# An mLSTM decoder layer: the output projection's second half of columns one chunk later, and operand transposes between halves of the first gate products

## Chip, cores and metric

One core of one Trainium2 chip. The metric is the device time in microseconds from the start to the end of one execution. The kernel before was run three times: median 2276.28 us.

## What is computed

One decoder layer (DEPTH = 1, so the mixer is the mLSTM), in float32, 2048 tokens of width 1024, then a SwiGLU feed-forward of width 2816:

```python
h = x
u = rmsnorm(h, mix_norm_g)
q, k, v, o_pre, if_pre = split(u @ w_in)                 # 8 heads, q and k of 64, v of 128
C, n, m = scan over chunks of the sequence               # matrix memory, stabilised by a running maximum
y = (merge_heads(_rms(num / max(|den|, exp(-m)))) * norm_g * sigmoid(o_pre)) @ w_out
h = h + y
u = rmsnorm(h, ffn_norm_g)
h = h + (silu(u @ w_gate) * (u @ w_up)) @ w_down
```

## The kernel before

Every engine's program is written out by hand, in order, with counting semaphores; no scheduler moves anything. The 2048 tokens are done as two halves of 1024 (`h` = 0, 1), and each half in stages:

- input projections (`project`, L1778), the products of normed rows with `w_in`, stored to HBM;
- the **chunk stage**, a loop over `TILES` = 8 chunks of 128 tokens (L1961 on TensorE, L1510 on VectorE, L990 on ScalarE, L712 on GpSimd);
- the **gate phase**, 11 groups of 14 products `feed(n, q, b)` (L1991), weights against the normed rows of the residual stream;
- the **down phase**, 77 products `drain(e)`.

Float32 precision comes from pairs of numbers: each operand is kept as a high part (a cast on ScalarE) and a low part (a subtraction on VectorE), and each product is three matmuls (low moving, high moving, low weights). The feed-forward products use a seven-product scheme over 2x2 blocks (`P1` to `P7`), so that besides the rows themselves some sums of rows are wanted as operands.

**A chunk on TensorE** (L1962 to L1977): `spread` (mask and decay arguments), `scores`, `weights` (its last four matmuls are transposes of k), then the first half of `out_tile(c - 2, 1)`, `turn_heads(c - 1)` (eight transposes of the normed heads), the second half of `out_tile(c - 2, 1)`, `state_sums`, `outputs`, `turn_v(c + 1)`, and `out_tile(c - 1, 0)`. `out_tile(c, jj, k0, k1)` is the output projection of chunk `c` for columns `512 * jj` on, 24 matmuls for all eight `k`, into bank `jj`.

**The heads of a chunk on the other engines.** After `outputs`, VectorE runs `head_scale_a`/`head_scale_b` (a chain of small operations that ends with `hrow`, L1489), TensorE turns `hrow`, VectorE multiplies with the gate (`gate_heads`, `og`, L1438), ScalarE casts that to `hg_hi` (L978), VectorE subtracts to `hg_lo` (L1443). `hg_hi` and `hg_lo` have two buffers. `add_out(c, jj)` (L1498) adds a finished `out_tile` to the residual rows `res`; when both column halves of a chunk are in, ScalarE sums squares (`norm2_sum`), GpSimd stores the rows to HBM (`store_h`, L710), and VectorE norms them (`norm2_rows`, L1150; for rows 0 to 5 it waits for that store).

**From the chunk stage to the gate phase** (L1979 to L1989, then inside `feed_group`, L2018, for the first group). The gate phase wants 16 operand units, `turn_unit(st + 1, n)`: units 0 to 3 are chunks 0 to 3 of the rows, units 4 to 15 are four triples made of row sums, parts A (4 + 4 transposes), B (4 + 4) and C (4). VectorE's `sum_early` (L1167, L1169) and GpSimd's `sum_late` (L632, L636) make the sums. A unit is transposed by TensorE (L1723), cast by ScalarE (`op_hi`, L781) and subtracted by VectorE (`op_lo`, L1174). Two PSUM places alternate, so from unit 4 on a transpose waits for an `op_lo` two units back:

```python
                if n >= 6 or (stage == 0 and n >= 2):
                    pe.wait_ge(op_lo_done, at + n - 1)
                elif n >= 4:
                    pe.wait_ge(op_lo_done, at + n - 2)
                elif stage % 2 and n == 3:
                    pe.wait_ge(op_lo_done, at + 1)
```

The first group's products 0 to 3 need units 0 to 3 only (`op_lo_done` 4); product 4 needs all parts B. The orders of VectorE and ScalarE in this stretch are L1568 to L1596 and L1021 to L1047. `feed_hi`/`feed_low` prepare a product's weights in `ring`, `feed_sums` their sums.

Of the kernel before, what the change touches and what calls it, by code (L numbers as in the profile page):

```python
# [5 lines left out]
F32 = mybir.dt.float32  # L6
# [79 lines left out]

def made_of(i, part=0):

    return i if i < 4 else 4 + 3 * (i - 4) + part


def mlstm_layer(nc, x, mix_norm_g, ffn_norm_g, w_gate, w_up, w_down, w_in, b_if, norm_g, w_out, out):
# [8 lines left out]
    with ExitStack() as ctx:  # L101
# [23 lines left out]
        r_q = region(32 * KB)  # L125
# [41 lines left out]
        hg_hi = [place(f"hg_hi{s}", r_q + 8 * KB * s, [P, KD, P], F32R) for s in range(2)]  # L167
        hg_lo = [place(f"hg_lo{s}", r_q + 8 * KB * s + 4 * KB, [P, KD, P], F32R) for s in range(2)]
# [205 lines left out]
        def part_of(stage, n):  # L374
            return ("BCA", "ABC")[stage % 2][(n - 4) % 3]

        def unit_for(stage, i, part):
            return made_of(i, ("BCA", "ABC")[stage % 2].index(part))
# [62 lines left out]
        def _(sp):  # L441
# [25 lines left out]
            for h in range(HALVES):  # L467
# [73 lines left out]
                sp.wait_ge(n_done, h * 8 + 8)  # L541
# [60 lines left out]
        def _(pool):  # L602
# [35 lines left out]
            for h in range(HALVES):  # L638
# [68 lines left out]
                def store_h(i):  # L707
                    pool.wait_ge(res_added, h * 16 + 2 * i + 2)
# [3 lines left out]
                for c in range(TILES):  # L712
                    if c >= 2:
                        store_h(c - 2)
                    squares(c)
                store_h(6)
                sum_late(st + 1, 0)
                sum_late(st + 1, 1)
                store_h(7)
                sum_late(st + 1, 2)  # L720
# [38 lines left out]
        def _(act):  # L759
# [42 lines left out]
            for h in range(HALVES):  # L802
# [171 lines left out]
                def hg_high(c):  # L974
                    act.wait_ge(hg_done, h * 8 + c + 1)
                    if c >= 2:
                        act.wait_ge(outp_done, h * 16 + 2 * (c - 2) + 2)
                    nc.scalar.copy(hg_hi[c % 2][:, :, :], og[c % 2][:, :, :]).then_inc(hghi_done, 1)  # L978

                def norm2_sum(i):  # L980
                    n = (st + 1) * TILES + i
                    act.wait_ge(res_added, h * 16 + 2 * i + 2)
# [7 lines left out]
                for c in range(TILES):  # L990
# [9 lines left out]
                    if c >= 2:  # L1000
                        norm2_sum(c - 2)
# [21 lines left out]
                feed_hi(0, 2)  # L1023
                norm2_sum(6)
                hg_high(7)
                act.wait_ge(outp_done, h * 16 + 15)
# [4 lines left out]
                act.wait_ge(hglo_done, h * 8 + 8)  # L1031
                norm2_sum(7)
                act.wait_ge(outp_done, h * 16 + 16)
                feed_hi(0, 3)
                for n in range(4, OP_UNITS):
                    op_hi(st + 1, n)
# [94 lines left out]
        def _(dve):  # L1131
# [102 lines left out]
            for h in range(HALVES):  # L1234
# [206 lines left out]
                def hg_low(c):  # L1441
                    dve.wait_ge(hghi_done, h * 8 + c + 1)
                    nc.vector.tensor_tensor(hg_lo[c % 2][:, :, :], og[c % 2][:, :, :],  # L1443
                                            hg_hi[c % 2][:, :, :].bitcast(F32), ALU.subtract).then_inc(hglo_done, 1)
# [659 lines left out]
```

## Time and profile before

| | |
|---|---|
| median of 3 runs | 2276.28 us (2270.1 to 2278.3) |
| the profiled execution, its own time | 2272.74 us |
| span of its instructions | 2271.1 us |
| TensorE matmuls busy | 2160.6 us (95%) |
| VectorE busy | 1459.3 us (64%) |
| ScalarE busy | 922.6 us (41%) |
| GpSimd busy | 280.4 us (12%) |
| mean granted TensorE clock | 0.980 |

The span runs from the first to the last instruction; the execution's own time is 1.64 us more. A matmul's end is modelled: a row of 0.39 us is followed by the next 0.23 us after its start when nothing is in the way, so "busy" is not the rate. Idle time stands in brackets behind a row, with what ended it. A granted clock of 1.0 is 2.4 GHz and 0.5 is 1.2 GHz.

### The profile page before, as it was taken

The page shows a single profiled execution, that of the slowest core. Times are in us where ns is not written, and L with a number is a line of the kernel's source. Part 1 is how long each engine was busy: PE and PEld are TensorE (multiplying, and loading weights), DVE is VectorE, ACT ScalarE, POOL GpSimd, SP SyncE. Part 2 cuts the span into 40 slices and gives each one's busy share as a digit, 9 for nine tenths or more (in the row PEclk, how much of TensorE's full clock was granted, in tenths as well). Part 3 has the DMA queues.
Part 4 walks back from the last instruction along what each step waited for, and adds up shares of the span by engine and source line. Part 5 has one row for each costly group of instructions (what it writes and reads, how often), then busy time and mean ns, then how long its engine had stood idle before and what let it go on. Part 6 is the DMA issues. An engine that isn't in the chain of part 4 may idle for free.

```text
span 2271.1 us, 29460 instructions
## 1 busy us (share of the span) xinstructions
PE 2160.6 (95%) x10440; PEld 1791.1 (79%) x10440; DVE 1459.3 (64%) x2274; ACT 922.6 (41%) x1670; POOL 280.4 (12%) x373
## 2 busy tenths in 40 slices
PE   5999989989999999999989999899799999999999
PEld 4778868867888888888867888688588888887887
DVE  7755456777565656579667553677766565656764
ACT  5433653334333333445434346533343333333443
POOL 3111110120010101100021111111201010101000
PEclk8999989999999999999999999899899999999999
DMA  4323372212323233864413334623032323257443
GB/s 140 96 90 112 102 263 95 97 47 74 113 93 115 92 115 127 298 228 114 149 63 107 107 104 138 218 102 103 19 112 98 111 97 111 97 179 247 148 120 117
DMA packets 200288, 281.56 MB, mean 124 GB/s; under 512 B 12912, under 2 KB 131696, under 8 KB 200176
## 3 DMA queue, kind: packets, MB, share of 16 engines
q1 hardware_dynamic: 171696, 183.07, 25.7%
q0 software_dynamic: 28480, 97.02, 12.1%
q8 instruction: 68, 1.11, 0.2%
q14 instruction: 44, 0.36, 0.0%
HBM read 197.73 MB, written 82.31 MB: 123 GB/s over the span
## 4 chain that ended last, share of the span: by engine, by line
PE 87%; DVE 7%; ACT 2%; issue 2%; DMA 1%; SPq 0%; POOL 0%; DVEq 0%; ACTq 0%; POOLq 0%
PE ps L2011 12%; PE ps L2013 12%; PE ps L2014 12%; PE ps L1802 6%; PE ps L1806 6%; PE ps L1804 6%; PE ps L2058 6%; PE ps L2062 6%; PE ps L2060 6%; PE ps L1716 2%; PE ps L1718 2%; PE ps L1717 2%; PE ps L1723 1%; PE ps L1924 1%; DVE u_lo L1174 1%
## 5 line engine op out<-in xcount | busy, mean ns | idle before, releaser
L1561 DVE TENSOR_TENSOR ring<-raw_f,ring 128x512 fp32r<-128x512 f32 x308 | 213.4, 694 | 190.0 <-ACT ring L1019 188.8
L2011 PE MATMUL ps<-u_lo,ring 128*128 128x512 f32 x704 | 275.1, 391 | 4.3 <-DVE u_lo L1174 4.3
L1019 ACT CAST ring<-raw_f 128x512 fp32r<-128x512 f32 x308 | 190.6, 622 | 212.0 <-PE ps L2014 196.8
L2013 PE MATMUL ps<-u_hi,ring 128*128 128x512 f32 x704 | 274.2, 389 | 0.0
L2014 PE MATMUL ps<-u_hi,ring 128*128 128x512 f32 x704 | 274.0, 389 | 0.0
L2058 PE MATMUL ps<-ring,ring 128*128 128x512 f32 x616 | 241.2, 392 | 3.3 <-DVE ring L1635 3.2
L2060 PE MATMUL ps<-ring,ring 128*128 128x512 f32 x616 | 240.4, 390 | 0.0
L2062 PE MATMUL ps<-ring,ring 128*128 128x512 f32 x616 | 240.2, 390 | 0.0
L2011 PE MATMUL ps<-t_op,ring 128*128 128x512 f32 x528 | 207.3, 393 | 5.9 <-DVE ring L1561 5.9
L2013 PE MATMUL ps<-t_op,ring 128*128 128x512 f32 x528 | 207.0, 392 | 0.0
L2014 PE MATMUL ps<-t_op,ring 128*128 128x512 f32 x528 | 206.9, 392 | 0.0
L1057 ACT CAST ring<-g_in 128x512 fp32r<-128x512 f32 x154 | 95.6, 621 | 222.3 <-PE ps L2062 210.3
L729 POOL DMA_DIRECT2D ops_hbm<-kept x154 | 83.3, 541 | 784.5 <-DVE kept L1654 584.9
L1629 DVE TENSOR_TENSOR ring<-g_in,ring 128x512 fp32r<-128x512 f32 x154 | 106.1, 689 | 112.7 <-ACT ring L1057 112.7
L1186 DVE TENSOR_TENSOR pring<-raw,pring 128x512 fp32r<-128x512 f32 x132 | 90.9, 691 | 128.1 <-ACT pring L798 127.3
L1802 PE MATMUL ps<-u_lo,pring 128*128 128x512 f32 x384 | 152.8, 398 | 9.0 <-ACT pkept L888 4.5
L1649 DVE TENSOR_TENSOR kept<-ps,kept 128x512 f32<-128x512 f32 x132 | 90.9, 688 | 109.3 <-PE ps L2014 109.3
L2011 PEld LDWEIGHTS ps<-u_lo,ring 128*128 128x128 f32 x704 | 132.5, 188 | 32.5 <-DVE u_lo L1174 5.1
L2014 PEld LDWEIGHTS ps<-u_hi,ring 128*128 128x128 f32 x704 | 132.3, 188 | 27.5
L2013 PEld LDWEIGHTS ps<-u_hi,ring 128*128 128x128 f32 x704 | 132.4, 188 | 27.1
L1804 PE MATMUL ps<-u_hi,pring 128*128 128x512 f32 x384 | 151.5, 395 | 0.0
L1806 PE MATMUL ps<-u_hi,pring 128*128 128x512 f32 x384 | 151.4, 394 | 0.0
(218 smaller groups left out, 4276.6 us busy)
## 6 DMA issues: line engine op xcount, KB each, us to landing
ops_hbm<-kept POOLq DMA_DIRECT2D x154, 256.0 KB, 2.4
g_in<-ops_hbm SPq DMA_DIRECT2D x154, 256.0 KB, 2.7
raw<-in_ml_w_in_dram SPq DMA_DIRECT2D x24, 1024.0 KB, 5.3
proj_hbm<-pkept POOLq DMA_DIRECT2D x96, 256.0 KB, 2.7
raw_f<-in_ffn_w_gate_dram SPq DMA_DIRECT2D x44, 512.0 KB, 4.7
raw_f<-in_ffn_w_up_dram SPq DMA_DIRECT2D x44, 512.0 KB, 4.7
b<-in_ffn_w_down_dram SPq DMA_DIRECT2D x88, 256.0 KB, 4.9
x_in<-in_x_dram SPq DMA_DIRECT2D x16, 512.0 KB, 5.9
```

The lines of the kernel that those rows point to most:

```text
L1019: nc.scalar.copy(four(ring[slot][:, 0, :]), feed_source(q, s)).then_inc(w_hi_done, 1)
L1561: nc.vector.tensor_tensor(four(ring[slot][:, 1, :]), feed_source(q, s), four(ring[slot][:, 0, :].bitcast(F32)), ALU.subtract).then_inc(w_l ...
L1629: nc.vector.tensor_tensor(ring[e % 3][:, 1, :], g_in[e % 4][:, :], ring[e % 3][:, 0, :].bitcast(F32), ALU.subtract).then_inc(ea_lo_done, 1)
L1802: pe.matmul(banks(bank), w[:, 0, now], moved(kind, 1, k), start=(fresh and k == 0), stop=False, skip_group_check=True)
L1804: pe.matmul(banks(bank), w[:, 0, now], moved(kind, 0, k), start=False, stop=False, skip_group_check=True)
L1806: last = pe.matmul(banks(bank), w[:, 1, now], moved(kind, 0, k), start=False, stop=(k == 3), skip_group_check=True)
L2011: pe.matmul(banks(bank), wh, moved(kind, 1, k), start=(fresh and k == 0), stop=False, skip_group_check=True)
L2013: pe.matmul(banks(bank), wh, moved(kind, 0, k), start=False, stop=False, skip_group_check=True)
L2014: last = pe.matmul(banks(bank), wl, moved(kind, 0, k), start=False, stop=(k == 3), skip_group_check=True)
L2058: pe.matmul(banks(bank + j), a[:, 0, now], w[:, 1, :], start=(fresh and n == 0), stop=False, skip_group_check=True)
L2060: pe.matmul(banks(bank + j), a[:, 0, now], w[:, 0, :], start=False, stop=False, skip_group_check=True)
L2062: last = pe.matmul(banks(bank + j), a[:, 1, now], w[:, 0, :], start=False, stop=(n == GROUPS - 1), skip_group_check=True)
```

## The change

The second half of columns of the output projection, `out_tile(c, 1)`, runs three chunks behind instead of two; for this the gated heads get a third pair of buffers (`hg_hi`, `hg_lo`, 8 KB per partition, behind `v1`), and every wait that counted `outp_done` or `res_added` goes by the new order, written as a table:

```diff
+OUT_ORDER = ([(0, 0), (1, 0)] + [pair for c in range(3, 8) for pair in ((c - 3, 1), (c - 1, 0))]
+             + [(5, 1), (6, 1), (7, 0), (7, 1)])
+def out_at(h, c, jj):
+    return h * 16 + OUT_ORDER.index((c, jj)) + 1
...
-        r_q = region(32 * KB)
+        r_q = region(32 * KB + 64)
...
+        hg_at = [r_q, r_q + 8 * KB, r_q + 24 * KB + 64]
...
-            return ("BCA", "ABC")[stage % 2][(n - 4) % 3]
+            return ("BCA", "BAC")[stage % 2][(n - 4) % 3]
```

TensorE in the chunk loop and after it:

```diff
-                    if c >= 2:
-                        out_tile(c - 2, 1, 0, 4)
+                    if c >= 3:
+                        out_tile(c - 3, 1, 0, 4)
...
-                out_tile(6, 1, 0, KD)
+                out_tile(5, 1, 0, KD)
                 turn_heads(7)
...
                 turn_unit(st + 1, 0)
                 turn_unit(st + 1, 1)
-                out_tile(7, 0, 0, KD)
+                out_tile(6, 1, 0, KD)
                 pe.wait_ge(hg_done, h * 8 + 8)
                 turn_unit(st + 1, 2)
+                out_tile(7, 0, 0, KD)
+                out_tile(7, 1, 0, 4)
                 turn_unit(st + 1, 3)
-                out_tile(7, 1, 0, KD)
+                out_tile(7, 1, 4, KD)
+                turn_unit(st + 1, 4)
```

In the first gate group the remaining units stand between halves of products 0 to 3 (`feed` takes a range of `k`):

```diff
-                        if first and q == 1:
-                            turn_unit(st + 1, 4)
-                            turn_unit(st + 1, 5)
...
+                        if first and q < 4:
+                            feed(n, q, b, 0, 2)
+                            turn_unit(st + 1, 5 + 2 * q)
+                            feed(n, q, b, 2, 4)
+                            turn_unit(st + 1, 6 + 2 * q)
+                            continue
                         if first and q == 4:
-                            for n_ in range(12, OP_UNITS):
-                                turn_unit(st + 1, n_)
+                            turn_unit(st + 1, 13)
+                            turn_unit(st + 1, 14)
+                            turn_unit(st + 1, 15)
```

Before product 4 TensorE now waits for 14 `op_lo`, before product 6 for 15. VectorE after the loop:

```diff
-                add_out(6, 1)
+                add_out(5, 1)
                 gate_heads(7)
                 hg_low(7)
-                norm2_rows(6)
-                op_lo(st + 1, 0)
-                op_lo(st + 1, 1)
+                norm2_rows(5)
+                add_out(6, 1)
                 sum_early(st + 1, 0)
                 sum_early(st + 1, 1)
+                norm2_rows(6)
                 add_out(7, 0)
+                op_lo(st + 1, 0)
+                op_lo(st + 1, 1)
+                sum_early(st + 1, 2)
                 op_lo(st + 1, 2)
                 op_lo(st + 1, 3)
-                sum_early(st + 1, 2)
                 add_out(7, 1)
+                op_lo(st + 1, 4)
                 norm2_rows(7)
+                feed_low(0, 3)
+                op_lo(st + 1, 5)
                 sum_early(st + 1, 3)
-                feed_low(0, 3)
```

ScalarE's order follows (a `norm2_sum(5)` ahead of `hg_high(7)`, `op_hi` of unit 4 ahead of `norm2_sum(7)`); GpSimd stores rows 5, 6 and 7 later; SyncE's load of the third and fourth gate weight blocks waits for `out_tile(5, 1)` instead of the last chunk's `outputs`. The instructions of every kind stay as many as they were; no DMA is added.

**TensorE, chunk 2 of the first half** (`qkc` is q and k, `hrow` the heads of chunk 1, `wo` the output weights). Before:

```order
L1881 MATMUL ps<-qkc_91 128x128 x8
L1891 MATMUL ps<-wint,pick 128x128 x4
L1895 MATMUL ps<-ident,qkc_91 128x128 x4
L1716 MATMUL ps<-wo_1_110,hg_hi_103 128x512
L1717 MATMUL ps<-wo_0_109,hg_hi_103 128x512
L1718 MATMUL ps<-wo_0_109,hg_lo_105 128x512
...
L1931 MATMUL ps<-ident,hrow 128x128 x8
```

and now:

```order
L1897 MATMUL ps<-qkc_91 128x128 x8
L1907 MATMUL ps<-wint,pick 128x128 x4
L1911 MATMUL ps<-ident,qkc_91 128x128 x4
L1947 MATMUL ps<-ident,hrow 128x128 x8
L1922 MATMUL ps<-v_0_96,kw 64x129 x8
L1936 MATMUL ps<-state,qw 128x129 x8
L1940 MATMUL ps<-v_0_96,dmat 128x129 x8
L1956 MATMUL ps<-ident,vtc 128x128 x8
L1732 MATMUL ps<-wo_1_110,hg_hi_104 128x512
L1733 MATMUL ps<-wo_0_109,hg_hi_104 128x512
L1734 MATMUL ps<-wo_0_109,hg_lo_107 128x512
```

Between the transposes of k and those of the heads stood 12 matmuls of `out_tile(0, 1)`, with 12 more behind the heads; now the heads follow directly, and the next `wo` rows are `out_tile(1, 0)`.

**TensorE, the first gate products** (`ring` holds weights, `res`, `t_second` the rows and sums of a unit). Before, behind product 0:

```order
L1723 MATMUL ps<-ident,res 128x128 x8
L1723 MATMUL ps<-ident,t_second_212 128x128 x4
L1723 MATMUL ps<-ident,res 128x128 x4
L2011 MATMUL ps<-u_lo,ring_122 128x512
L2013 MATMUL ps<-u_hi,ring_122 128x512
L2014 MATMUL ps<-u_hi,ring_122 128x512
...
L1723 MATMUL ps<-ident,res 128x128 x12
L1723 MATMUL ps<-ident,t_second_213 128x128 x4
L1723 MATMUL ps<-ident,res 128x128 x4
```

and now, from the middle of product 0 on:

```order
L1739 MATMUL ps<-ident,res 128x128 x8
L2031 MATMUL ps<-u_lo,ring_123 128x512
L2033 MATMUL ps<-u_hi,ring_123 128x512
L2034 MATMUL ps<-u_hi,ring_123 128x512
...
L1739 MATMUL ps<-ident,res 128x128 x4
L2031 MATMUL ps<-u_lo,ring_124 128x512
L2033 MATMUL ps<-u_hi,ring_124 128x512
L2034 MATMUL ps<-u_hi,ring_124 128x512
...
L1739 MATMUL ps<-ident,t_second_215 128x128 x4
L1739 MATMUL ps<-ident,res 128x128 x4
```

Where two or three units stood in a row between whole products of 12 matmuls, one unit now stands behind every six matmuls.

**VectorE, from the last `add_out` of the stage on** (L1174, now L1186, is `op_lo`; L1167 and L1169, now L1179 and L1181, are `sum_early`; L1498, now L1510, is `add_out`; the `nv` rows and the one behind them are the norm of rows 7). Before:

```order
L1498 TENSOR_TENSOR res<-ps,res 128x512
L1136 TENSOR_SCALAR nv<-nv 128x1
L1141 TENSOR_SCALAR nv<-nv 128x1
L1144 SCALAR_TENSOR_TENSOR nv<-nv 128x1
L1150 SCALAR_TENSOR_TENSOR xn_0_115<-res,nv,gain_114 128x1024
L1167 TENSOR_TENSOR res<-xn_0_115,res 128x512
L1169 TENSOR_TENSOR t_second_215<-xn_0_115,res 128x512
L1561 TENSOR_TENSOR ring_124<-raw_f_118,ring_124 128x512
L1174 TENSOR_TENSOR u_lo<-ps,u_hi 128x8x128
L1174 TENSOR_TENSOR t_op<-ps,t_op 128x2x4x128
```

and now, from `op_lo` of units 2 and 3 on:

```order
L1186 TENSOR_TENSOR u_lo<-ps,u_hi 128x8x128 x2
L1510 TENSOR_TENSOR res<-ps,res 128x512
L1186 TENSOR_TENSOR t_op<-ps,t_op 128x2x4x128
L1148 TENSOR_SCALAR nv<-nv 128x1
L1153 TENSOR_SCALAR nv<-nv 128x1
L1156 SCALAR_TENSOR_TENSOR nv<-nv 128x1
L1162 SCALAR_TENSOR_TENSOR xn_0_117<-res,nv,gain_116 128x1024
L1573 TENSOR_TENSOR ring_126<-raw_f_120,ring_126 128x512
L1186 TENSOR_TENSOR u_lo<-ps,u_hi 128x8x128
L1179 TENSOR_TENSOR res<-xn_0_117,res 128x512
L1181 TENSOR_TENSOR t_second_217<-xn_0_117,res 128x512
```

`op_lo` of unit 4 now stands ahead of the norm of rows 7, and that of unit 5 ahead of the last sums.

## Rows read from the trace of the kernel before

**Rows 1.** The page: span, busy time, chain by engine

```profile
span 2271.1 us, 29460 instructions
...
PE 2160.6 (95%) x10440; PEld 1791.1 (79%) x10440; DVE 1459.3 (64%) x2274; ACT 922.6 (41%) x1670; POOL 280.4 (12%) x373
...
PE 87%; DVE 7%; ACT 2%; issue 2%; DMA 1%; SPq 0%; POOL 0%; DVEq 0%; ACTq 0%; POOLq 0%
```

**Rows 2.** Stretches: length, PE, PEld, DVE, ACT, POOL busy (count), clock, DMA share, GB/s

```profile
361.88:382.12 20.24, 20.24 (x148) 17.22 (x147) 14.57 (x28) 7.39 (x18) 2.50 (x2) 1.00 0.30 106
...
462.20:524.00 61.80, 45.98 (x242) 37.94 (x240) 44.66 (x59) 23.21 (x36) 13.54 (x10) 0.94 0.04 17
...
529.70:600.00 70.30, 70.30 (x311) 58.18 (x310) 46.98 (x72) 28.23 (x49) 7.61 (x14) 1.00 0.36 113
1581.50:1643.20 61.70, 45.76 (x242) 37.74 (x240) 44.56 (x58) 23.14 (x36) 13.52 (x10) 0.93 0.04 18
```

**Rows 3.** Timeline of PE behind the loop: start, duration, what, [idle before, releaser]

```profile
473.84 0.61 PE L1716 MATMUL ps<-wo,hg_hi 128*128 128x512 f32 x1 [3.38 <-DVE hg_lo L1443]
474.25 0.63 PE L1717 MATMUL ps<-wo,hg_hi 128*128 128x512 f32 x1
...
477.24 0.51 PE L1718 MATMUL ps<-wo,hg_lo 128*128 128x512 f32 x1
...
483.55 1.09 PE L1723 MATMUL ps<-ident,res 128*128 128x128 f32 x8 [1.49 <-DVE u_lo L1174]
484.40 0.48 PE L1716 MATMUL ps<-wo,hg_hi 128*128 128x512 f32 x1
...
492.26 0.50 PE L2011 MATMUL ps<-u_lo,ring 128*128 128x512 f32 x1 [2.15 <-DVE u_lo L1174]
...
503.53 0.63 PE L1723 MATMUL ps<-ident,res 128*128 128x128 f32 x4 [3.75 <-issue]
504.62 1.83 PE L1723 MATMUL ps<-ident,res 128*128 128x128 f32 x8 [0.46 <-DVE t_op L1174]
506.24 1.06 PE L1723 MATMUL ps<-ident,t_second 128*128 128x128 f32 x4
...
523.94 0.47 PE L2011 MATMUL ps<-t_op,ring 128*128 128x512 f32 x1 [2.94 <-DVE ring L1561]
```

**Rows 4.** Waits of PE, 462 to 530: in total, times, longest

```profile
PE ps L1723 <- DVE u_lo L1174: 2.2, 2, 1.5
...
PE ps L1723 <- DVE t_op L1174: 1.4, 3, 0.5
```

**Rows 5.** Timeline of PE in chunk 2

```profile
344.96 0.48 PE L1716 MATMUL ps<-wo,hg_hi 128*128 128x512 f32 x1
...
356.31 0.47 PE L1716 MATMUL ps<-wo,hg_hi 128*128 128x512 f32 x1
```

**Rows 6.** Timeline of ACT in chunk 2

```profile
343.10 2.17 ACT L955 ACTIVATE dmat<-ps,colt 128x128 f32<-128x128 f32 x8 [1.23 <-PE ps L1869]
350.14 1.05 ACT L978 CAST hg_hi<-og 128x1024 fp32r<-128x1024 f32 x1 [4.87 <-DVE og L1438]
```

**Rows 7.** Timeline of DVE: chunk 2, the end of chunk 7, and behind the loop

```profile
346.05 1.21 DVE L1431 TENSOR_TENSOR dmat<-ps,dmat 128x1024 f32<-128x1024 f32 x1
...
463.73 1.22 DVE L1489 TENSOR_TENSOR hrow<-num,hv 128x1024 f32<-128x1024 f32 x1
...
484.54 0.68 DVE L1167 TENSOR_TENSOR res<-res 128x512 f32<-128x512 f32 x1
...
485.86 1.78 DVE L1167 TENSOR_TENSOR res<-res 128x512 f32<-128x512 f32 x1
...
497.89 1.29 DVE L1150 SCALAR_TENSOR_TENSOR xn<-res,nv,gain 128x1024 f32<-128x1024 f32 x1
...
502.22 1.21 DVE L1174 TENSOR_TENSOR u_lo<-ps,u_hi 128x1024 fp32r<-128x1024 f32 x1
```

**Rows 8.** Landing of the stores of rows to HBM, all 16

```profile
DMA to landing us min/median/max: 2.9/3.9/12.8
```

More of the change, by code:

```diff
@@ L166, in mlstm_layer @@
         num = place("num", r_c + 28 * KB, [P, HEADS, VW], F32)
-        hg_hi = [place(f"hg_hi{s}", r_q + 8 * KB * s, [P, KD, P], F32R) for s in range(2)]
-        hg_lo = [place(f"hg_lo{s}", r_q + 8 * KB * s + 4 * KB, [P, KD, P], F32R) for s in range(2)]
+        hg_at = [r_q, r_q + 8 * KB, r_q + 24 * KB + 64]
+        hg_hi = [place(f"hg_hi{s}", at, [P, KD, P], F32R) for s, at in enumerate(hg_at)]
+        hg_lo = [place(f"hg_lo{s}", at + 4 * KB, [P, KD, P], F32R) for s, at in enumerate(hg_at)]
         wo = [[place(f"wo{jj}_{part}", r_u + 16 * KB * jj + 32 * KB * part, [P, KD, NB], F32R) for part in range(2)]
@@ L1030, in _ @@
                 op_hi(st + 1, 3)
-                act.wait_ge(hglo_done, h * 8 + 8)
+                op_hi(st + 1, 4)
                 norm2_sum(7)
-                act.wait_ge(outp_done, h * 16 + 16)
+                act.wait_ge(outp_done, out_at(h, 7, 1))
                 feed_hi(0, 3)
-                for n in range(4, OP_UNITS):
+                for n in range(5, OP_UNITS):
                     op_hi(st + 1, n)
@@ L1520, in _ @@
                             split_out(1, k)
-                    if c >= 2:
-                        add_out(c - 2, 1)
+                    if c >= 3:
+                        add_out(c - 3, 1)
                     if c:
@@ L1969, in _ @@
                         turn_heads(c - 1)
-                    if c >= 2:
-                        out_tile(c - 2, 1, 4, KD)
+                    if c >= 3:
+                        out_tile(c - 3, 1, 4, KD)
                     state_sums(c)
@@ L2008, in feed @@
                     fresh = kind in ("P1", "P2", "P5")
-                    for k in range(4):
+                    for k in range(k0, k1):
                         wh, wl = ring[slot][:, 0, k * P:k * P + P], ring[slot][:, 1, k * P:k * P + P]
@@ L2015, in feed @@
                                          skip_group_check=True)
-                    last.then_inc(fed, 1)
+                    if k1 == 4:
+                        last.then_inc(fed, 1)
                 def feed_group(n, b, is_second=False):
```

74 lines of the change are left out of this document (35 added, 39 removed).

## The prediction

> **What bounds the kernel now.** I read the page first: TensorE's matmuls are busy for 95% of the span and hold 87% of the chain of work that ended last, VectorE 7% [rows 1]. So time is won only where TensorE stands idle or runs at the lower clock, and VectorE matters where TensorE waits for it. Then the table of stretches [rows 2]: a chunk from the third on takes 20.24 us and TensorE is busy in all of it; the gate phase from 529.70 on too, 311 matmuls in 70.30 us, 0.226 us each. Between them lies the way from chunk stage to gate phase, 462.20 to 524.00, where TensorE is busy for 45.98 of 61.80 us, at a mean clock of 0.94; the second half has the same stretch with 45.76 of 61.70 us. This is the place of the change.
>
> The timeline of that stretch [rows 3] and the waits in it [rows 4] name nine idle times: 3.38 us until the low part of chunk 7's heads is there, 1.49 and 0.74 (together the 2.2 of the waits on `u_lo`), 2.15 ahead of product 0, 3.75 ahead of unit 6, 1.4 in three waits for `t_op`, 2.94 ahead of product 4. Sum 15.8 us. The 3.75 stands as "issue"; by the program unit 6 waits for `op_lo` of unit 4, which is the row that starts at 502.22 and ends at 503.43 [rows 7], just ahead of 503.53. A matmul's row is 0.39 long where the next starts after 0.23, so each idle time costs about 0.16 more than its bracket: nine times, 1.4. There is a lower clock too: after the 3.38 idle eight matmuls stand 0.43 apart instead of 0.23 (0.63 long, 474.25 to 477.24), 1.6 us late; after the 3.75 idle eight transposes take 1.62 us to the next row (504.62 to 506.24), where at 483.55 eight took 0.85, and as many more follow: 1.5 us. That is 2.4 GHz against 1.2 GHz. Together the stretch holds 15.8 + 1.4 + 3.1 = **20.3 us** above its work, per half.
>
> **The change, part by part.**
>
> *Chunk 2 loses its cover.* `out_tile(0, 1)`, 24 matmuls, 5.45 us, leaves chunk 2 and every later one slides by a chunk, so chunks 3 to 7 hold the same work as before and stay at 20.24. In chunk 2 TensorE comes to the heads at 344.96 [rows 5], but the eight exponentials on the decay arguments, whose banks the heads overwrite, end at 343.10 + 2.17 = 345.27 [rows 6]: idle 0.5. The heads themselves are ready. Next check: `out_tile(1, 0)`, at 356.31 before, is reached at about 351.3. It needs the low part of chunk 1's heads: VectorE ends `dmat` at 347.26 [rows 7], gates for 1.2 (348.5), ScalarE casts 1.05 [rows 6] (349.6), VectorE subtracts (350.9). 0.4 us of slack. So 0.5, at least 0.3, and if the chain of heads were 2 us later, 2.5.
>
> *The work behind the loop.* The stretch now starts 5.45 - 0.5 = 5.0 us earlier and holds 5.45 us more. The heads of chunk 7, before ready at 463.73 + 1.22 = 464.95 [rows 7], come 5.0 earlier too, at 460, and TensorE asks for them behind `out_tile(5, 1)` at 462.7. While gate, cast and subtraction run (until about 468.8), TensorE has two units and `out_tile(6, 1)` until 470.7: the **3.38 is gone**, and with it the lower clock behind it.
>
> *Unit 3 and product 0.* Late next is VectorE. After `out_tile(6, 1)` it has an `add_out` (0.68), four sums, the norm of rows 6 (1.29 and its small steps, 2.0), `add_out(7, 0)` and `op_lo` of unit 0 (1.21) before unit 3 may start. The sums take 0.68 each alone and 1.78 where GpSimd works beside them [rows 7], so 2.7 to 4.9 in all. The chain is 7.3 to 9.5 us, from 470.7 to 478.0 to 480.2, with four hand-overs of 0.1 at most 480.6; TensorE is there at 470.7 + 0.85 + 5.45 + 2.72 = 479.8. Idle 0 to 0.8 by this, I take 1.0 since ScalarE's casts of rows sit between. Unit 3 and the last 12 output matmuls then run without a hole, unit 4 too, and `op_lo` of unit 3 is done at about 485.5, when TensorE reaches product 0. **1.49 becomes 1.0, 2.15 becomes 0.**
>
> *Units 5 to 12 between halves of products.* A unit takes 0.85, its cast 1.05, its subtraction 1.21: 3.1, and 3.3 with hand-overs. The unit two behind starts after unit n, six matmuls (1.36), the unit between (0.44 or 0.85), six matmuls: 4.0 or more. So these waits are covered as long as VectorE is free at once. `op_lo` of unit 4 now stands ahead of the norm of rows 7, which takes the **3.75** away with its lower clock; but `op_lo` of unit 5 still stands behind that norm, and unit 7 waits for it: by the same sums VectorE is done at 492.0, TensorE ready at 491.2. Idle 0.9.
>
> *Units 13 to 15 and product 4.* These have no matmuls between them. Unit 13 waits for unit 11: 3.3 against 0.85 + 1.36 + 0.44, idle 0.5. Unit 15 waits for unit 13: 3.3 against 1.7, idle 1.5. Product 4 comes behind the last casts, the first two copies and the weights' low part, and was late by 2.94; now two sums of weights stand ahead of the last two `op_lo`, so I take 3.5.
>
> *Small things.* The first matmul after transposes is 0.48 long instead of 0.39 [rows 3]; four more such changes per half, 0.4. SyncE's load of two weight blocks now waits for the end of `out_tile(5, 1)`, at 462.7, and its blocks are first summed near 498. The store of rows 5 is issued at 464.8 and wanted at 468.8, 4.0 us later; stores land in 3.9 at the median, 12.8 at most [rows 8]. I take 0.3 of wait on VectorE, covered, since the next `add_out` waits until 470.8.
>
> **The sum, per half:** 20.3 taken away; given back 0.5 + 1.0 + 0.9 + 0.5 + 1.5 + 3.5 + 0.4 = 8.3. Gain 12.0, twice 24 us. The profiled execution took 2272.74 us, so 2248.7 against it. The median of the runs is 3.5 us above that execution; halfway between, I predict **2250 us**.
>
> **A rule that speaks against it.** In the trace the eight transposes at 483.55 and the matmuls behind them run at the upper clock, and the two falls came after idle times of more than 3 us [rows 3]. The Trainium skill, "TensorE: Matmul & The Clock Gate", Part 4 (PE-mode transpose), says that transposes do not count as activity for the clock gate the way matmuls do. By that rule groups of six matmuls with transposes between them could run at 1.2 GHz; the time of that is the third rival.
>
> **Rivals.**
>
> 1. *VectorE becomes the bound of the stretch.* It is busy for 44.7 of the 61.8 us, and gets an `add_out` and a norm more: 47.3. My sum squeezes the stretch to 61.7 + 5.0 - 12.0 = 54.7 us, with only 7.4 us of VectorE idle where it had 17. If its chains to ScalarE keep 12.7 us idle, the stretch is 60 and the gain 6.7 per half: **2259**. For it: each `op_lo` waits for a cast. Against: the long idle times of VectorE were caused by ScalarE waiting for whole output tiles, which now come earlier. 20%.
> 2. *The lost cover in chunk 2 and the short slack of the store.* If the heads' chain costs 2.5 in chunk 2 and a store of rows 5 lands after 12.8 us (8.8 late, of which 2 are covered), a half loses up to 8.8: gain 3 per half, **2266**, no change by measure. Against: only one store in 16 was that long. 10%.
> 3. *The lower clock, ending slower.* From unit 3 on, 60 matmuls of output and gate products and 88 transposes are mixed. At 1.2 GHz each of these matmuls costs 0.2 more (12.0 us) and eight transposes 0.77 more (8.5 us): 20 per half, 8 more than the gain, so **2289**. It decides from about 12 us lost per half, that is when more than half of the mixed stretch runs at the lower level. For it: the falls at 474 and 504. Against: both followed idle times of 3.4 and 3.7 us, and none longer than 1.5 is left before unit 15. 4%.
> 4. *All new idle times stay covered*, gain 17 to 20 per half: **2235**. 5%.
>
> **Chances.** My forecast, 2240 to 2259 about 2250, has 61%. A change below 0.5% (11.4 us) can't be told from none in this kernel; from 2276.3 the bounds are 2264.9 and 2287.7. Faster takes the forecast, rival 4, nearly all of rival 1: 83%. Same: rival 2 and the edge of rival 1, 13%. Slower: 4%. The range, 2239 to 2265, leaves out rival 4, rival 3 and most of rival 2.
>
> **What would show it.** Right: the chunk from 341.6 takes about 15.3; no idle time at the first row of `out_tile(7, 0)`; `op_lo` of unit 4 starts about 486.6; product 4 starts about 511 with some 3 us of idle ahead of it; PE's idle time between loop and product 4 is 7 us per half; both halves alike. Wrong: waits of 1 us or more at most of units 5 to 12 (rival 1), matmuls 0.43 apart between 480 and 505 (rival 3), idle ahead of `out_tile(1, 0)` (rival 2).

## The result, and the profile after

| | before | after |
|---|---|---|
| median of the runs | 2273.43 us (2268.7 to 2278.3, 8 runs) | 2282.41 us (2279.26 to 2289.88, 8 runs) |
| the profiled execution | 2272.74 us | 2279.28 us |
| span | 2271.1 us | 2277.5 us |
| mean granted TensorE clock | 0.980 | 0.982 |

The ratio is 1.0039, with a 95% interval of 1.0025 to 1.0054: no faster, 0.4% slower, inside the 0.5% that counts as no change, and above the range of 2239 to 2265. The prediction of 2250 was wrong.

The page of the kernel after: span, busy time, chain by engine.

```profile
span 2277.5 us, 29462 instructions
...
PE 2183.0 (96%) x10440; PEld 1787.0 (78%) x10440; DVE 1458.5 (64%) x2274; ACT 922.8 (41%) x1670; POOL 279.8 (12%) x373
...
PE 87%; DVE 7%; issue 2%; ACT 2%; DMA 2%; SPq 0%; DVEq 0%; ACTq 0%; POOLq 0%
```

Against [rows 1] the same 10440 matmuls are busy for 22.4 us more. Nothing in the change adds a matmul or lengthens one on purpose, and the mean granted clock is no lower (0.982 against 0.980), so the loss is not a wait: each matmul takes longer.

Now the kernel after at the place of the change and behind it. The timeline of PE (TensorE): the first matmul of chunk 2 and of chunk 3, then every idle time above 0.4 us between the loop and product 4, with two of the matmuls behind the first of them.

```profile
344.89 0.39 PE L1882 MATMUL ps<-mask,ident_b 128*128 128x512 bf16 x1
...
359.99 0.39 PE L1882 MATMUL ps<-mask,ident_b 128*128 128x512 bf16 x1
...
486.35 1.09 PE L1739 MATMUL ps<-ident,res 128*128 128x128 f32 x8 [2.81 <-DVE u_lo L1186]
...
487.80 0.63 PE L1734 MATMUL ps<-wo,hg_lo 128*128 128x512 f32 x1
...
490.78 0.54 PE L1732 MATMUL ps<-wo,hg_hi 128*128 128x512 f32 x1
...
499.00 0.66 PE L1739 MATMUL ps<-ident,t_second 128*128 128x128 f32 x4 [0.83 <-DVE u_lo L1186]
...
511.10 0.66 PE L1739 MATMUL ps<-ident,t_second 128*128 128x128 f32 x4 [0.55 <-DVE u_lo L1186]
...
514.56 0.66 PE L1739 MATMUL ps<-ident,res 128*128 128x128 f32 x4 [1.49 <-DVE t_op L1186]
...
518.33 0.69 PE L2031 MATMUL ps<-t_op,ring 128*128 128x512 f32 x1 [3.11 <-DVE ring L1573]
```

The nine idle times of [rows 3], 15.8 us, have become five, 8.8 us. That is the part of the change that the prediction was about, and it came. What came with it stands in the gate and down phases, which the change doesn't touch. First two stretches of 100 us of the kernel before (gate phase, down phase), then the same of the kernel after, and for the change's own place its stretch. The columns are those of [rows 2], and the number in brackets behind the first busy time is that of matmuls started:

```profile
600.00:700.00 100.00, 100.00 (x443) 82.79 (x442) 59.13 (x92) 36.91 (x64) 8.66 (x16) 1.00 0.33 105
940.00:1040.00 100.00, 100.00 (x443) 82.79 (x442) 75.47 (x119) 44.65 (x81) 2.84 (x4) 1.00 0.68 235
```

```profile
600.00:700.00 100.00, 100.00 (x437) 81.83 (x436) 59.60 (x92) 36.85 (x64) 8.36 (x17) 1.00 0.33 105
940.00:1040.00 100.00, 100.00 (x430) 80.60 (x429) 73.00 (x114) 43.47 (x79) 2.84 (x4) 1.00 0.68 233
...
464.89:518.33 53.44, 44.64 (x247) 37.08 (x246) 42.92 (x54) 22.91 (x36) 13.78 (x11) 0.97 0.15 50
```

TensorE is busy in all of each 100 us, at the full granted clock, in both kernels, and yet starts 437 and 430 matmuls instead of 443 and 443. The pace has changed. It can be read by product in the timeline of PE in one gate group, the first matmuls of products 0 to 4, 9 and 10 of the kernel after (a product has 12):

```profile
701.84 0.40 PE L2031 MATMUL ps<-u_lo,ring 128*128 128x512 f32 x1
...
704.64 0.40 PE L2031 MATMUL ps<-u_lo,ring 128*128 128x512 f32 x1
...
707.44 0.40 PE L2031 MATMUL ps<-u_lo,ring 128*128 128x512 f32 x1
...
710.24 0.39 PE L2031 MATMUL ps<-u_lo,ring 128*128 128x512 f32 x1
...
712.99 0.40 PE L2031 MATMUL ps<-t_op,ring 128*128 128x512 f32 x1
...
726.83 0.39 PE L2031 MATMUL ps<-t_op,ring 128*128 128x512 f32 x1
...
729.55 0.39 PE L2031 MATMUL ps<-u_lo,ring 128*128 128x512 f32 x1
```

and products 0 to 2 of the same group in the kernel before:

```profile
705.19 0.39 PE L2011 MATMUL ps<-u_lo,ring 128*128 128x512 f32 x1
...
707.91 0.39 PE L2011 MATMUL ps<-u_lo,ring 128*128 128x512 f32 x1
...
710.63 0.39 PE L2011 MATMUL ps<-u_lo,ring 128*128 128x512 f32 x1
```

Before, a product takes 2.72 us (226.7 ns a matmul), and all 14 do. After, products 0, 1 and 2 take 2.80 (233.3 ns), product 3 takes 2.75, and product 9 takes 2.72 as before. The paces come back in the same order in every group. A product's pace thus goes with its place in the group, not with the time at which it runs.

Where the time went in the two profiled executions, in us. Projections and down phases are counted from the start of their first matmul to that of the third from the end. "Way" is from there in the input projections to product 4, and holds the chunk stage and the place of the change; "gate" is from product 4 to the down phase. The small handovers between down phase and next projections (0.7) are left out.

| | proj. 1 | way 1 | gate 1 | down 1 | proj. 2 | way 2 | gate 2 | down 2 |
|---|---|---|---|---|---|---|---|---|
| before | 274.6 | 225.7 | 409.7 | 214.1 | 268.4 | 226.3 | 410.5 | 213.3 |
| after | 277.3 | 217.4 | 415.1 | 219.6 | 273.4 | 215.2 | 416.3 | 214.9 |

The ways became 8.3 and 11.1 us shorter, the gate phases 5.4 and 5.8 longer, projections and down phases 14.8 longer together. The gain is there, and more than all of it is given back in work that "stayed as it was".

Two of these columns hold more than the change. A way has waits at its start that differ from execution to execution (the last section); from the first of the `negm`, `pick` matmuls of chunk 2 to product 4 it is 182.3 and 182.3 us before, and 173.4 and 171.7 after, 8.9 and 10.6 less. A down phase has waits at its products 9 to 11 whose chain in the trace of the kernel before leads to a load from HBM (`g_in`, 7.6 us): 4.6 us more than the usual pace in the second half before, nothing in either half after. By the pace alone its 924 matmuls would have grown by 924 * 6.6 ns = 6.1 us, an estimate from the paces above.

### The profile page after: what moved, and what is told of

Same layout as the page of the kernel before. It is cut to its first block, busy times and chain, and to the rows that moved or that the text cites. A ratio compares the mean times of both kernels' runs of the same rounds, so it can differ in the third digit from the quotient of the medians.

```text
span 2277.5 us, 29462 instructions
## 1 busy us (share of the span) xinstructions
PE 2183.0 (96%) x10440; PEld 1787.0 (78%) x10440; DVE 1458.5 (64%) x2274; ACT 922.8 (41%) x1670; POOL 279.8 (12%) x373
## 4 chain that ended last, share of the span: by engine, by line
PE 87%; DVE 7%; issue 2%; ACT 2%; DMA 2%; SPq 0%; DVEq 0%; ACTq 0%; POOLq 0%
PE ps L2031 12%; PE ps L2034 12%; PE ps L2033 12%; PE ps L2077 6%; PE ps L2081 6%; PE ps L2079 6%; PE ps L1818 6%; PE ps L1820 6%; PE ps L1822 6%; PE ps L1732 2%; PE ps L1734 2%; PE ps L1733 2%; PE ps L1739 1%; PE ps L1940 1%; PE ps L1835 1%
## 5 line engine op out<-in xcount | busy, mean ns | idle before, releaser
L2077 PE MATMUL ps<-ring,ring 128*128 128x512 f32 x616 | 244.0, 396 | 0.5 <-DVE ring L1651 0.5
L2081 PE MATMUL ps<-ring,ring 128*128 128x512 f32 x616 | 243.5, 395 | 0.0
L2079 PE MATMUL ps<-ring,ring 128*128 128x512 f32 x616 | 243.5, 395 | 0.0
```

The lines of the kernel that those rows point to most:

```text
L2077: pe.matmul(banks(bank + j), a[:, 0, now], w[:, 1, :], start=(fresh and n == 0), stop=False, skip_group_check=True)
L2079: pe.matmul(banks(bank + j), a[:, 0, now], w[:, 0, :], start=False, stop=False, skip_group_check=True)
L2081: last = pe.matmul(banks(bank + j), a[:, 1, now], w[:, 0, :], start=False, stop=(n == GROUPS - 1), skip_group_check=True)
```

## The experiments

What did the change do to products that it doesn't touch? It moved their operands. The third buffer of gated heads is `region(32 * KB + 64)` instead of `region(32 * KB)`. The regions are laid one behind the other (`r_u`, `r_v`, `r_q`, `r_a`, `r_b`, `r_c`), so that `r_a`, `r_b`, `r_c` and the small tiles stand 64 bytes further on in each partition, while `r_u`, `r_v` and `r_q` stay. In the kernel before the first five are 65536, 33024, 32768, 16384 and 16384 bytes long, all multiples of 256, and so the starts of any two differ by a multiple of 256. A product's weights, the stationary operand, lie in slot `q % 7` of `ring`: slots 0 and 1 in `r_b`, 2 in `r_a`, 3 to 6 in `r_q`. Its moving operand is `u` in `r_u`, or `t_op` in `r_c` (products 4, 5, 8, 9) or `r_v`. In the down phase both operands are slots: stationary 0 to 2, moving 3 to 5.

The theory was **placement**: where the two operands of a matmul stand relative to each other sets its pace. Its rival was **order**: the new order of stores and loads disturbs TensorE (rows stored later, weight blocks loaded at other times).

**Shift alone, and another shift.** First the kernel before with nothing but the 64 bytes:

```diff
-        r_q = region(32 * KB)
+        r_q = region(32 * KB + 64)
```

> The kernel before with one edit: 64 bytes more behind region r_q, so that r_a, r_b, r_c and all small tiles lie 64 bytes further, at addresses that are multiples of 64 and no longer of 128. Order of work untouched. Theory A (the shift slows matmuls whose tiles are shifted): 12-matmul products take 2.80 us instead of 2.72 in the down phase (233.3 ns per matmul against 226.7), the gate phase 7 us and the down phase 6 us longer per half, in all 25 to 40 us over the kernel before, near 2305. Theory B (the slower pace comes from the new order, of instructions or of transfers): the pace stays 226.7 and the time at 2273.

Measured: 2298.72 us (4 runs) against 2271.29 (17 runs), ratio 1.0117 (1.0101 to 1.0133). Its stretch from 600 to 700 us, in the gate phase:

```profile
600.00:700.00 100.00, 100.00 (x437) 81.72 (x436) 56.27 (x86) 36.70 (x64) 8.12 (x15) 1.00 0.32 103
```

437 matmuls, as in the kernel after, and its gate phases last 415.1 and 415.9 us, as there. By product its paces in the gate phase are those of the kernel after within 0.1 ns. No instruction was moved, so the rival falls: 64 bytes cost 27 us by themselves.

The kernel after with `region(32 * KB + 128)`:

> The changed kernel with 128 bytes instead of 64 behind r_q, so that every region starts at a multiple of 128 again; order of work as in the change. Theory A: pace back to 226.7 ns everywhere, and what the new order saves between chunk stage and gate phase is left, 2245 to 2258. Theory B: as the changed kernel, 2282.

Measured: 2276.67 us (12 runs), ratio 1.0018 (1.0008 to 1.0029). This was a miss. 128 bytes are almost as bad as 64 in pace: the down phase's starts are 2.79 us apart for 12 matmuls, 232.5 ns. So the placement theory stood, but its first rule (any multiple of 128 will do) was wrong.

**Which pairs matter.** The kernel before with only `r_c` and what is behind it shifted:

```diff
-        r_b = region(16 * KB)
+        r_b = region(16 * KB + 64)
```

> The kernel before with 64 bytes behind r_b: only r_c (t23_op, a moving operand of products P6 and P7) and the small tiles are shifted; the weights' ring and pring stay in place. If the stationary side is what counts: 2273 to 2278, products 0 to 2 of a gate group and the down phase at 226.7. If any shifted operand counts: P6 and P7 products (4 of 14) slow, the down phase at 226.7, 2280 to 2285.

Measured: 2281.94 us (4 runs), ratio 1.005 (1.0031 to 1.0069). Its stretch from 600 to 700 us:

```profile
600.00:700.00 100.00, 100.00 (x440) 82.27 (x439) 56.38 (x86) 37.32 (x64) 8.14 (x15) 1.00 0.33 104
```

440 matmuls, half of the fall, and it is where the theory puts it: the products whose moving operand is in `r_c` run at 228.9 to 230.3 ns, those on `u` at 226.7 except right behind them (products 6 and 10, 230.8), and the down phase, none of whose operands is in `r_c`, at 226.7.

Both edits at once (`r_a` and `r_b` shifted by 64, `r_c` by 128):

> The kernel before with 64 bytes behind r_q and 64 more behind r_b: r_a and r_b (three of seven weight buffers, the ring's stationary side in the down phase) are shifted, r_c and the small tiles are in place again. If the stationary side counts: down phase at 233.3, products 0, 1, 2, 7, 8, 9 of a gate group slow, 2290 to 2305. If it is r_c or the small tiles: 2273.

Measured: 2300.17 us (4 runs), ratio 1.0125 (1.0108 to 1.0142), and 436 matmuls in the stretch of 600 to 700 us. Hardly worse than the 64 bytes alone. The expectation calls `r_c` "in place again"; it stands 128 bytes off, and products 4 and 5, which the expectation does not list as slow, ran at 232.7 and 233.3 ns. By the differences below they should.

**The difference, not the address.** The second form of the theory: the pace hangs on the address of the stationary operand less that of the moving one, modulo 256. Two tests. The kernel before with every region 64 bytes further on, so that all addresses change and no difference does:

```diff
-        top = [base]
+        top = [base + 64]
```

> The kernel before with every region 64 bytes further: no tile at a multiple of 128, but all differences between tiles unchanged. If the relation between operands counts (A2): pace 226.7 ns and 2271. If each operand's own address counts (A1): pace 233 ns in nearly all products, 2305 or more.

Measured: 2271.42 us (10 runs), ratio 0.9998 (0.9988 to 1.0008). Its stretch from 600 to 700 us is the one of before, 443 matmuls:

```profile
600.00:700.00 100.00, 100.00 (x443) 82.84 (x442) 59.52 (x91) 36.85 (x63) 8.68 (x16) 1.00 0.33 105
```

And the kernel after with its order untouched and 256 bytes instead of 64:

```diff
-        r_q = region(32 * KB + 64)
+        r_q = region(32 * KB + 256)
```

> The changed kernel with 256 bytes instead of 64 behind r_q. In the kernel before every region starts at the same remainder modulo 256 (128); with 64 or 128 more behind r_q the regions behind it do not. Theory A2 (the slower pace comes from a stationary and a moving operand whose addresses differ modulo 256): pace 226.7 ns in all products, and the saving of the new order is left, 2245 to 2256. Theory A3 (any move of the regions costs, or a coarser remainder, 512 or more, counts): slower pace as before, 2270 to 2280.

Measured: 2258.44 us (2256.29 to 2263.01, 6 runs) against 2272.21 (22 runs), ratio 0.9938 (0.9926 to 0.9951). Its stretch from 600 to 700 us:

```profile
600.00:700.00 100.00, 100.00 (x443) 82.81 (x442) 63.73 (x98) 36.13 (x63) 10.14 (x19) 1.00 0.33 106
```

All 14 products are back at 226.7 ns, and the change is worth 14 us; the time is 2.4 above the 2245 to 2256 that was written. The same order costs 24 us more with 64 bytes than with 256 (2282.4 against 2258.4; 23 by the ratios, as the two were timed beside different executions of the kernel before). That is why the result is not a gain. One pair of operands is still 64 bytes off in this kernel: the third buffer of gated heads has a `+ 64` of its own inside `r_q`, and `out_tile(5, 1)`, which reads it, runs at 233.5 ns, where `out_tile(6, 1)` at the same place of the kernel before runs at 226.6.

Two more sizes, on the kernel before: 192 bytes and 32 bytes in `r_q`.

> The kernel before with 192 bytes behind r_q. Runs so far, by the difference of stationary minus moving address modulo 256: 0 gives 226.7 ns per matmul, 64 gives 233.3, 128 gives 232.5 to 233.3, and a moving operand 64 further (difference 192) gives 229 to 230. If the difference modulo 256 is what counts: the down phase (stationary 192, moving 0) at 229 to 230, products 4 and 5 (stationary 0, moving 192, difference 64) at 233, time 2285 to 2295, under the 2298.7 of 64 bytes. If only which side is shifted counts: down phase 233, time as with 64 bytes.

> The kernel before with 32 bytes behind r_q. If lines of 64 bytes matter, an address in the middle of one is as bad or worse: 2295 or more. If the loss grows with the difference in small steps, half of that of 64: near 2285. If 32 bytes fall into the same line: 2271.

Measured for 192: median 2286.49 us (2285.48 to 2295.91, 4 runs), ratio 1.0053 (1.0034 to 1.0072). The profiled run is the slowest of the four. For 32: 2300.51 us (4 runs), ratio 1.0121 (1.0101 to 1.0142). The down phase is where every matmul has the same difference of operands. Its timeline for 192 bytes, 12 matmuls from row to row:

```profile
999.97 0.39 PE L2062 MATMUL ps<-ring,ring 128*128 128x512 f32 x1
...
1002.72 0.39 PE L2062 MATMUL ps<-ring,ring 128*128 128x512 f32 x1
```

2.75 us, against 2.72 before and 2.80 with 64 bytes. In the gate phase of the kernel with 192 bytes it is turned round: product 4, with weights in `r_q` and rows in `r_c`, has a difference of -192, that is 64 modulo 256, and takes 233.3 ns a matmul. All paces together, each the median of (start to start of the next product)/12, of products in a row with the same difference:

| stationary less moving address, mod 256 | ns a matmul | where |
|---|---|---|
| 0 | 226.7 | before; all shifted by 64; 256 bytes |
| 32 | 233.3 | down phase, 32 bytes |
| 64 | 233.3 | down phase and products 0, 1 of after; product 5 of 192 bytes |
| 128 | 232.5, 233.3 | down phase; product 5, 128 bytes |
| 192 | 228.9 | down phase, 192 bytes; product 5 of after |
| 224 | 233.3 | product 5 of 32 bytes |

So 32 bytes cost as much as 64, either way round, and the cost is not symmetrical: 192 (64 the other way round) costs a third of what 64 does. The 226.7 holds for differences that are a multiple of 256; `r_u` and `r_q` differ by an odd multiple of 256 at no cost. A product's own difference is not all of it. In the kernel after products 3, 6 and 8 have a difference of 0, stand behind a product that has not, and take 229.1, 230.8 and 230.2 ns; on average over all groups product 6 stays at 227 only from its eleventh matmul on. Sizes between those of the table were not tried, and nothing here shows what in the chip makes it.

**Which half of the change brings the gain?** Now with the placement mended. The kernel with 256 bytes, but units 5 to 12 in twos and threes ahead of whole products 1, 2 and 3, no longer between halves:

```diff
-                        if first and q < 4:
-                            feed(n, q, b, 0, 2)
-                            turn_unit(st + 1, 5 + 2 * q)
-                            feed(n, q, b, 2, 4)
-                            turn_unit(st + 1, 6 + 2 * q)
-                            continue
+                        if first and q == 1:
+                            turn_unit(st + 1, 5)
+                            turn_unit(st + 1, 6)
...
+                        if first and q == 3:
+                            turn_unit(st + 1, 10)
+                            turn_unit(st + 1, 11)
+                            turn_unit(st + 1, 12)
```

> As e5 (changed order, 256 bytes), with the second part of the change undone on TensorE: units 5 and 6 stand ahead of whole product 1, 7 to 9 ahead of 2, 10 to 12 ahead of 3. If the halves carry part of the gain: unit 6, 8, 9, 11, 12 wait 0.5 to 1.5 us each again, 3 to 6 us over e5 in all. If the gain lies in the output projection and VectorE's order alone: within 2 us of e5.

Measured: 2259.29 us (5 runs), ratio 0.9938 (0.9925 to 0.9951): within the noise of the kernel with halves. From chunk 2 to product 4 it takes 173.6 and 173.5 us, against 173.4 and 173.1 with halves. So most of the gain lies in the rest of the change. That the halves add nothing isn't shown, though: between loop and product 4 TensorE stands idle for 10.2 and 10.1 us, against 8.8 with halves, and the profiled execution made up for it, since its clock stayed at 1.00 behind the wait of unit 3 in both halves (2.85 and 2.70 us idle), where that of the kernel with halves fell. The 1.3 us of idle time per half is what the halves are worth by the trace, and the medians can't tell 3 us from nothing.

And the halves alone, on the kernel before: units 4 to 11 between halves of products 0 to 3, everything else as it was (`feed` takes a range of `k` for it, as in the change).

```diff
-                        if first and q == 1:
-                            turn_unit(st + 1, 4)
-                            turn_unit(st + 1, 5)
...
+                        if first and q < 4:
+                            feed(n, q, b, 0, 2)
+                            turn_unit(st + 1, 4 + 2 * q)
+                            feed(n, q, b, 2, 4)
+                            turn_unit(st + 1, 5 + 2 * q)
+                            continue
```

> The kernel before with only the second part: units 4 to 11 between halves of products 0 to 3, units 12 to 15 ahead of product 4; output projection, buffers and VectorE's order as before. The waits of 3.75 us on the low part of unit 4 and of 3.38 on the heads stay. Expected 3 to 6 us under the kernel before, 2266 to 2269; if the halves do nothing alone, 2271.

Measured: 2280.34 us (11 runs), ratio 1.0033 (1.002 to 1.0047). Not a gain but a small loss, a miss. Its timeline of PE between product 0 and product 4 (the waits of most of a microsecond), and its stretch from 462 us to product 4:

```profile
503.37 1.12 PE L1723 MATMUL ps<-ident,res 128*128 128x128 f32 x4 [5.05 <-DVE u_lo L1174]
...
519.21 0.66 PE L1723 MATMUL ps<-ident,res 128*128 128x128 f32 x4 [1.60 <-DVE t_op L1174]
...
521.20 1.11 PE L1723 MATMUL ps<-ident,t_second 128*128 128x128 f32 x4 [0.90 <-DVE t_op L1174]
...
527.02 0.47 PE L2012 MATMUL ps<-t_op,ring 128*128 128x512 f32 x1 [3.00 <-DVE ring L1561]
```

```profile
462.00:527.02 65.02, 47.33 (x243) 38.91 (x242) 44.69 (x60) 22.95 (x36) 13.56 (x10) 0.90 0.04 17
```

Unit 6 still waits for `op_lo` of unit 4, which stands where it stood on VectorE, behind the norm of rows 7. It starts at 503.37 as it did at 503.53 [rows 3]. TensorE now only comes to it six matmuls earlier and waits 5.05 us instead of 3.75, and those six matmuls come after it. The granted clock of the stretch is 0.90 where it was 0.94 [rows 2]. Product 4 is 3.1 us later, and from chunk 2 to product 4 it takes 185.3 and 185.5 us where it took 182.3. To reach a wait earlier, without making what it waits for earlier, moves cover from ahead of it to behind it.

**A version that beats both.** The five idle times that are left name what is late. Unit 3 waits 2.81 for `op_lo` of unit 0. VectorE (DVE) in the kernel after, ahead of it:

```profile
473.38 0.15 DVE L1148 TENSOR_SCALAR nv<-nv 128x1 f32<-128x1 f32 x1 [1.15 <-DMA h_hbm<-res]
...
476.59 0.69 DVE L1181 TENSOR_TENSOR t_second<-res 128x512 f32<-128x512 f32 x1
477.20 1.78 DVE L1179 TENSOR_TENSOR res<-res 128x512 f32<-128x512 f32 x1
479.01 1.67 DVE L1181 TENSOR_TENSOR t_second<-res 128x512 f32<-128x512 f32 x1
...
481.09 2.15 DVE L1156 SCALAR_TENSOR_TENSOR nv<-nv 128x1 f32<-128x1 f32 x1
483.28 1.28 DVE L1162 SCALAR_TENSOR_TENSOR xn<-res,nv,gain 128x1024 f32<-128x1024 f32 x1
484.48 0.68 DVE L1510 TENSOR_TENSOR res<-ps,res 128x512 f32<-128x512 f32 x1
485.08 2.35 DVE L1186 TENSOR_TENSOR u_lo<-ps,u_hi 128x1024 fp32r<-128x1024 f32 x2
```

The norm of rows 6 (480.6 to 484.5) isn't wanted by anyone at that moment, and `op_lo` of unit 0, in the last row, could go ahead of it. Product 4 waits 3.11 for the low part of its weights, which stands behind `op_lo` of all 16 units. The kernel with 256 bytes, with these two moved:

```diff
+                op_lo(st + 1, 0)
                 norm2_rows(6)
                 add_out(7, 0)
-                op_lo(st + 1, 0)
...
-                for n in range(10, 14):
-                    op_lo(st + 1, n)
+                op_lo(st + 1, 10)
+                feed_low(0, 4)
+                op_lo(st + 1, 11)
+                op_lo(st + 1, 12)
                 feed_sums(0, 3)
-                for n in range(14, OP_UNITS):
+                for n in range(13, OP_UNITS):
                     op_lo(st + 1, n)
+                feed_sums(0, 4)
```

and ScalarE's `feed_hi(0, 4)` and the first two copies of kept results up to the casts of units 10 and 12.

> e5 (changed order, 256 bytes) with the two waits that are left taken on: VectorE does the low part of unit 0 ahead of the norm of rows 6, and ScalarE and VectorE make product 4's weights and the first two copies between units 10 to 13 instead of behind unit 15. If these waits are what unit 3 (2.8 us) and product 4 (3.1 us) stand for: both go, about 6 us per half, 2245 to 2249. If something else is right behind them (ScalarE's casts, the next product's weights): half of it, 2252.

Measured: 2248.11 us (2243.68 to 2249.29, 5 runs) against 2274.06 (9 runs), ratio 0.9883 (0.9865 to 0.9901). All idle times above 0.4 us of PE between loop and product 5:

```profile
485.15 0.50 PE L2038 MATMUL ps<-u_lo,ring 128*128 128x512 f32 x1 [2.39 <-DVE u_lo L1190]
...
504.35 0.66 PE L1746 MATMUL ps<-ident,t_second 128*128 128x128 f32 x4 [0.55 <-DVE u_lo L1190]
...
507.80 0.66 PE L1746 MATMUL ps<-ident,res 128*128 128x128 f32 x4 [1.49 <-DVE t_op L1190]
...
515.62 0.47 PE L2038 MATMUL ps<-u_lo,ring 128*128 128x512 f32 x1 [1.50 <-DVE kept L1672]
```

Unit 3 and product 4 no longer wait. Part of the first comes back as 2.39 us ahead of product 0, and 1.50 of the second as a wait for a kept copy inside the gate phase. The move took something else away that wasn't planned: the small operation of the norm of rows 6, 2.15 us in the kernel after at 481.09, no longer runs beside GpSimd's sums.

```profile
478.29 0.16 DVE L1160 SCALAR_TENSOR_TENSOR nv<-nv 128x1 f32<-128x1 f32 x1
```

From chunk 2 to product 4 it now takes 168.6 us in both halves, 4.8 and 4.5 less than with 256 bytes alone, less than the 6 per half that was written. The medians lie 10.3 us apart, the two profiled executions 14.3, of which 5.0 lie in the other stages, where nothing was moved.

## Why the prediction was wrong, by its own steps

- **The step that failed** is the premise of the sum, nowhere argued as a whole, that everything outside the place of the change keeps its time. The part *Chunk 2 loses its cover* holds that chunks 3 to 7 stay at 20.24, and the sum goes from "Gain 12.0, twice 24 us" straight to the time of the execution. The `+ 64` in the diff was costed at nothing, without a sentence on what it moves. The runs showed 27 us for it on the kernel before, and 24 us between 64 and 256 bytes on the changed one. No rival had it, and the range, which ends at 2265, did not hold the 2282.4. Of the 7560 matmuls of the three large phases most became up to 6.6 ns slower.
- **Chunk 2**: right. From 344.89 to 359.99 us are 15.10, predicted 20.24 - 5.45 + 0.5 = 15.3.
- **The 3.38 gone**: right, no idle time there. **3.75 and 2.15 gone**: right.
- **Unit 3**: predicted 1.0, measured 2.81, the mis-sized term. The chain was summed to start at 470.7 and to need 7.3 to 9.5 us. It had in addition 1.15 of waiting for the store of rows 5, which was called covered, and a small operation on 128x1 that took 2.15 instead of 0.16 beside GpSimd. And the clock fell behind this idle time, which the sum had not: the starts from 487.80 to 490.78 stand 0.43 apart, 1.2 GHz, which costs 1.5 us. In the second half it did not fall behind nearly the same wait:

```profile
1611.88 1.09 PE L1739 MATMUL ps<-ident,res 128*128 128x128 f32 x8 [2.71 <-DVE u_lo L1186]
...
1613.04 0.39 PE L1733 MATMUL ps<-wo,hg_hi 128*128 128x512 f32 x1
```

- **Units 5 to 12**: 0.83 where 0.9 was said, all others covered. **Units 13 to 15**: 0.55 and 1.49, said 0.5 and 1.5. **Product 4**: 3.11, said 3.5.
- **The sum**: it took away 0.16 for the edge of each idle time, but gave none back. Given back are 8.8 of idle, 0.8 for its five edges, 1.5 of clock, 0.3 in chunk 2 and 0.4 of changes between kinds (an estimate of the prediction), 11.8 of the 20.3. That leaves 8.5 per half; from chunk 2 to product 4 the traces show 8.9 and 10.6, and with 256 bytes 8.9 and 9.2. Predicted were 12.0. With this error alone the time would have been about 2257, which the range holds. The times of the rivals lack the 1.8 us that the forecast adds for the median of the runs.
- **VectorE as the bound (rival 1)** was near in size (6.7 per half, 2259) but not in kind: its chain to ScalarE cost nothing at most of the units. What cost in between was one operand behind a norm, and that could be moved.
- **The lower clock (rival 3)** did not come. Mixed transposes and matmuls from 491.4 to 514.0:

```profile
491.40:514.00 22.60, 20.29 (x126) 16.92 (x124) 15.62 (x20) 11.58 (x16) 3.60 (x3) 1.00 0.06 24
```

  The granted clock is 1.00 in all of it. Between the loop and product 4 matmuls ran at the lower clock only behind the idle 2.81, and in the second half none did. The Trainium skill ("TensorE: Matmul & The Clock Gate", Part 4, on the PE-mode transpose) holds that transposes don't count as activity as matmuls do. This mixture of one unit to six matmuls doesn't show it.
- The **reason given for the gain** was half right. It named both parts of the change. The run with whole products shows that the later output projection and the new orders of VectorE and ScalarE bring most of it; what the units between halves bring is too small for the runs to tell from nothing.

## What to carry to other kernels

- When a change touches the size of a buffer, look at what is laid out behind it. Before any explanation by waits, count the instructions in a stretch in which the engine is busy throughout, before and after: a pace that changed shows there at once, and nowhere in the lists of waits.
- Here the operands of a matmul had to stand a multiple of 256 bytes apart in their partitions. Where a kernel's tiles are placed by hand, keep every region a multiple of 256 bytes long, and cost a pad as an edit of its own.
- To bring a consumer forward gains only if its producer comes forward too. Find the one operation that is late on the other engine, and move what nobody waits for behind it.

## What the runs showed of the hardware that was not expected

- A 128x512 matmul on float32 pairs starts 226.7, 228.9, 232.5 or 233.3 ns after the one before, by the difference of its operands' addresses modulo 256 (0; 192; 128; 32, 64 and 224), at the same granted clock of 1.00. Where everything is shifted together nothing changes.
- The slower pace reaches into the next product. Product 3 of the kernel after has a difference of 0 and took 2.75 us, product 6, behind one with a difference of 192, took 2.77, more than that one itself, and product 9, behind another product with difference 0, took 2.72.
- Whether the granted clock falls behind an idle time of one length differs between executions. Behind the 3.38 to 3.40 us at the low part of chunk 7's heads it fell in both halves of the kernel before, in the first half alone where all was shifted by 64, and in the second alone with 192 bytes. A fall there is worth about 1.5 us, and it is part of what tells two executions apart.
- Beside GpSimd a VectorE operation on 128x512 took 1.78 us instead of 0.69, and one on 128x1 2.15 instead of 0.16. The Trainium skill ("GPSIMD Engine Reference", 1. Specifications) says that the two engines share their SBUF interfaces and contend where a VectorE instruction has two SBUF inputs, which agrees with the rows. GpSimd (POOL) at that time:

```profile
476.65 1.78 POOL L641 TENSOR_TENSOR res<-res 128x512 f32<-128x512 f32 x1 [7.19 <-DVE res L1179]
...
481.93 1.28 POOL L645 TENSOR_TENSOR res<-res,t_second 128x512 f32<-128x512 f32 x1
```

  The small operation ends at 481.09 + 2.15 = 483.24, just behind the second of these (481.93 + 1.28 = 483.21), so it reads as having waited that sum out. The long VectorE sum ends at 477.20 + 1.78 = 478.98, 0.55 us behind the first of them (478.43), about its own time, which reads the same. Two small operations with one input, at 480.60 and 480.78, took their usual 0.14 and 0.27 while GpSimd was at a sum.
- TensorE's wait for `vtc`, a load from HBM early in each chunk stage, was 1.0 to 5.4 us a half in the profiled executions of the different kernels, without order by the kernel. With the waits of the down phase (0 to 4.6 us a half), these are a few of the microseconds by which executions differ. The verdicts rest on the medians and on the paces, not on them.
